# A decoder block on one core: the output is turned back on TensorE, and the projection stage goes from three pairs of PSUM banks to two

## What is computed

```
mod = silu(c) @ w_ada + b_ada          # shift, scale and gate, twice
h   = rms_norm(x) * (1 + scale1) + shift1
out_a = sparse attention(h)            # (512, 512)
out_b = gated linear recurrence(h)     # (512, 512)
merged = sigmoid(gate_a) * (out_a @ w_proj_a) + sigmoid(gate_b) * (out_b @ w_proj_b)
x   = x + gate1 * (merged @ w_out)
h2  = rms_norm(x) * (1 + scale2) + shift2
y   = square(relu(h2 @ w_mlp1 + b_mlp1)) @ w_mlp2 + b_mlp2
return x + gate2 * y                   # (1, 512 tokens, 1024 channels)
```

## Time and profile before

| | us |
|---|---|
| median of 3 runs | 870.14 |
| lowest and highest | 869.37, 870.98 |
| the profiled execution, its own time | 870.14 |
| its span in the profile | 868.3 |
| TensorE busy in the span | 827.7 (95%) |
| VectorE busy | 460.3 (53%) |
| ScalarE busy | 324.6 (37%) |

### The profile page before, as it was taken

The page is one execution under the profiler, slowest core; times in us unless marked ns, Lnnn a source line. Parts: engine busy times, 40 slices in busy tenths (PEclk is TensorE's granted clock), DMA queues, the critical chain, the costliest instruction groups (busy, mean ns, idle before and its releaser), DMA issues.

```text
span 868.3 us, 10841 instructions
## 1 busy us (share of the span) xinstructions
PE 827.7 (95%) x3919; PEld 666.8 (77%) x3919; DVE 460.3 (53%) x714; ACT 324.6 (37%) x495; POOL 222.1 (26%) x127
## 2 busy tenths in 40 slices
PE   2699899989999999999999989999999999999998
PEld 1567667878878887676888878888888888888886
DVE  3942478995788976667596656942111122220000
ACT  2643525244253335656433234444111144441110
POOL 4023423440000000000000205544444434445440
PEclk9789989999999999999999989999999999999999
DMA  9913312331222223245474722733333333333320
GB/s 353 293 52 92 97 49 73 88 90 40 74 51 56 65 73 98 79 134 153 123 226 145 232 73 81 234 97 97 97 97 97 97 97 97 97 97 97 97 97 25
DMA packets 141625, 95.74 MB, mean 110 GB/s; under 512 B 8214, under 2 KB 134804, under 8 KB 140564
## 3 DMA queue, kind: packets, MB, share of 16 engines
q1 hardware_dynamic: 140032, 95.05, 37.0%
q10 hardware_dynamic: 1556, 0.20, 0.2%
HBM read 93.13 MB, written 2.10 MB: 110 GB/s over the span
## 4 chain that ended last, share of the span: by engine, by line
PE 82%; DVE 12%; ACT 3%; issue 1%; DMA 1%; ACTq 1%; DVEq 0%
PE bank L1272 17%; PE bank L1273 17%; PE bank L1274 17%; PE bank L1422 3%; PE bank L1424 3%; PE bank L1423 3%; DVE score L980 3%; DVE top L978 3%; PE bank L1442 2%; PE bank L1614 2%; PE bank L1615 2%; PE bank L1616 2%; PE bank L1396 2%; PE bank L1300 2%; DVE rt_k L940 2%; PE bank L1398 1%
## 5 line engine op out<-in xcount | busy, mean ns | idle before, releaser
L439 POOL TENSOR_TENSOR w_lo<-w_raw,w_hi 128x1024 fp32r<-128x1024 f32 x82 | 203.5, 2483 | 322.3 <-ACT w_hi L510 322.3
L1272 PE MATMUL bank<-h_hi,w_hi 128*128 128x512 f32 x464 | 184.8, 398 | 5.3 <-DVE h_lo L918 4.8
L1273 PE MATMUL bank<-h_lo,w_hi 128*128 128x512 f32 x464 | 182.5, 393 | 0.0
L1274 PE MATMUL bank<-h_hi,w_lo 128*128 128x512 f32 x464 | 182.4, 393 | 0.0
L510 ACT ACTIVATE w_hi<-w_raw 128x1024 fp32r<-128x1024 f32 x126 | 132.6, 1052 | 133.0 <-PE bank L1274 121.4
L1272 PEld LDWEIGHTS bank<-h_hi,w_hi 128*128 128x128 f32 x464 | 88.2, 190 | 29.6 <-issue 7.6
L1274 PEld LDWEIGHTS bank<-h_hi,w_lo 128*128 128x128 f32 x464 | 88.2, 190 | 18.7
L1273 PEld LDWEIGHTS bank<-h_lo,w_hi 128*128 128x128 f32 x464 | 88.3, 190 | 17.9 <-issue 0.2
L1272 PE MATMUL bank<-u_hi,w_hi 128*128 128x512 f32 x256 | 99.7, 389 | 0.0
L1274 PE MATMUL bank<-u_hi,w_lo 128*128 128x512 f32 x256 | 99.6, 389 | 0.0
L1273 PE MATMUL bank<-u_lo,w_hi 128*128 128x512 f32 x256 | 99.6, 389 | 0.0
(11 more groups left out here) (231 smaller groups left out, 1207.4 us busy)
## 6 DMA issues: line engine op xcount, KB each, us to landing
w_raw<-in_w_mlp SPq DMA_DIRECT2D x128, 256.0 KB, 3.0
w_raw<-in_w_in SPq DMA_DIRECT2D x88, 256.0 KB, 3.4
ada_raw<-in_w_ada SPq DMA_DIRECT2D x8, 1024.0 KB, 9.0
ada_even<-in_w_ada SPq DMA_DIRECT2D x16, 512.0 KB, 4.6
ada_odd<-in_w_ada SPq DMA_DIRECT2D x16, 512.0 KB, 4.6
w_raw<-in_w_out SPq DMA_DIRECT2D x16, 256.0 KB, 3.2
x_nat<-in_x SPq DMA_DIRECT2D x4, 512.0 KB, 6.2
w_raw<-in_w_proj_a SPq DMA_DIRECT2D x8, 256.0 KB, 3.9
```

Source lines behind the costliest of these rows:

```text
L439: nc.gpsimd.tensor_tensor(w_lo[:, s], w_raw[:, s], w_hi[:, s].bitcast(F32), ALU.subtract).then_inc(lo_ready, 1)
L1272: mm(bank[b][:], w_hi[:, slot, j], rhs_hi(i), start=f, stop=False)
L1273: mm(bank[b][:], w_hi[:, slot, j], rhs_lo(i), start=False, stop=False)
L1274: end = mm(bank[b][:], w_lo[:, slot, j], rhs_hi(i), start=False, stop=l)
```

## The change

Two things are changed.

1. **The output.** The result tensor is now (1, 512 tokens, 1024 channels). Each of the 8 blocks of `xT` is turned by four 128x128 transposes on TensorE into bank 2 or 3 (`turn_back`), ACT copies the bank into a new buffer `o_stage` of two places (L841 of the changed kernel), and SP writes it: 128 partitions x 4 token blocks x 128 channels, so 512 pieces of 512 bytes where there were 128 rows of 2 KB. The last block is added on DVE in one piece, and ACT issues no DMA any more. `o_stage` lies in memory that nothing uses by then. The transposes of blocks 0 and 1 come after unit `j = 0` of `down(3)`, those of 2 and 3 after `j = 1`, of 4 and 5 after `j = 2`, of 6 and 7 after `j = 3`.
2. **The projection.** Banks 2 and 3 drop out of the rotation; blocks alternate between the pair 4, 5 and the pair 6, 7. `proj_taken` is gone. TensorE now asks, before block `m` from `m = 2` on, that `merged_ready` has come to `m - 1`, that is, that DVE has finished all of block `m - 2`, its `h_lo` included.

```diff
-    out_v = out.rearrange("(m p) t -> m p t", p=P)
+    out_v = out[0].rearrange("(b p) (m n) -> m p b n", p=P, n=P)
...
+        o_stage = place("o_stage", RL + 8 * KB, [P, 2, TB, P])
...
-        PROJ_BANK = [4, 6, 2]
...
-            for m in range(KC - 1):
-                sp.wait_ge(lin_evac, E_2[1] + m + 1)
-                sp.dma_start(out_v[m], xT[:, m]).then_inc(out_written, 16)
-            sp.wait_ge(lin_evac, E_2[1] + KC)
-            sp.dma_start(out_v[KC - 1][:, 0:T // 2], xT[:, KC - 1, 0:T // 2]).then_inc(out_written, 16)
-            sp.wait_ge(out_written, 16 * KC)
+            for m in range(KC):
+                sp.wait_ge(out_staged, m + 1)
+                sp.dma_start(out_v[m], o_stage[:, m % 2]).then_inc(out_written[m % 2], 16)
+            for b in range(2):
+                sp.wait_ge(out_written[b], 16 * KC // 2)
...
-            act.wait_ge(lin_evac, E_2[1] + KC + 1)
-            act.dma_start(out_v[KC - 1][:, T // 2:T], xT[:, KC - 1, T // 2:T]).then_inc(tail_written, 16)
-            act.wait_ge(tail_written, 16)
+            for m in range(KC):
+                act.wait_ge(y_turned, m + 1)
+                if m >= 2:
+                    act.wait_ge(out_written[m % 2], 16 * (m // 2))
+                nc.scalar.activation(o_stage[:, m % 2], bank[2 + m % 2][:].rearrange("p (b n) -> p b n", b=TB),
+                                     ACT.Copy).then_inc(out_staged, 1)
...
             for m in range(KC):
                 dve.wait_ge(group_done, G[U_P + m + 1])
-                b = PROJ_BANK[m % 3]
+                b = 4 + 2 * (m % 2)
                 sa, sb, mh, ml = sig_a[:, m], sig_b[:, m], h_hi[:, m], h_lo[:, m]
                 v.tensor_tensor(sa, bank[b][:], sa, ALU.mult)
                 dve.wait_ge(sigb_ready, m + 1)
-                v.tensor_tensor(sb, bank[b + 1][:], sb, ALU.mult).then_inc(proj_taken, 1)
-                dve.wait_ge(proj_taken, m + 1)
+                step(v.tensor_tensor(sb, bank[b + 1][:], sb, ALU.mult))
...
-                        for t in ((slice(0, T // 2), slice(T // 2, T)) if m == KC - 1 else (slice(0, T),)):
-                            v.scalar_tensor_tensor(out=xT[:, m, t], in0=bank[m % 2][:, t], scalar=GATE2[:, m:m + 1],
-                                                   in1=xT[:, m, t], op0=ALU.mult, op1=ALU.add
-                                                   ).then_inc(lin_evac, 1)
+                        v.scalar_tensor_tensor(out=xT[:, m], in0=bank[m % 2][:], scalar=GATE2[:, m:m + 1],
+                                               in1=xT[:, m], op0=ALU.mult, op1=ALU.add).then_inc(lin_evac, 1)
...
             for m in range(2, KC):
-                if m >= 3:
-                    pe.wait_ge(proj_taken, m - 2)
+                pe.wait_ge(merged_ready, m - 1)
                 pe.wait_ge(lo_ready, U_P + m + 1)
...
-            down(3)
+            def turn_back(m):
+                pe.wait_ge(lin_evac, E_2[1] + m + 1)
+                if m >= 2:
+                    pe.wait_ge(out_staged, m - 1)
+                for b in range(TB):
+                    end = nc.tensor.transpose(bank[2 + m % 2][:, b * P:(b + 1) * P],
+                                              xT[:, m, b * P:(b + 1) * P], ident[:])
+                end.then_inc(y_turned, 1)
+
+
+            for j in range(4):
+                down(3, (j,))
+                for m in (2 * j, 2 * j + 1):
+                    if m < KC - 2 or j == 3 and m < KC - 1:
+                        turn_back(m)
+            turn_back(KC - 1)
```

More of the change, by code:

```diff
@@ L235, in hybrid_block @@
             sem("sqo_ready"), sem("sqo_added"), sem("orow_summed"), sem("orow_ready"), sem("orow_spread"))
-        proj_taken = sem("proj_taken")
         sigb_ready = sem("sigb_ready")
@@ L239, in hybrid_block @@
         u_hi_ready = sem("u_hi_ready")
-        out_written, tail_written = sem("out_written"), sem("tail_written")
+        y_turned, out_staged = sem("y_turned"), sem("out_staged")
+        out_written = [sem("out_written0"), sem("out_written1")]
         assert G[U_1[0]] % 2 == 0 and G[U_1[1]] % 2 == 0
@@ L1609, in proj_blocks @@
                 n = U_P + m
-                b = PROJ_BANK[m % 3] + j0 // AC
+                b = 4 + 2 * (m % 2) + j0 // AC
                 rhs_hi, rhs_lo = (oa_hi, oa_lo) if j0 < AC else (ob_hi, ob_lo)
@@ L1779 @@
                                    kind="ExternalInput").ap())
-    _, T, D = inputs["x"].shape
-    out = nc.dram_tensor("out", (D, T), F32, kind="ExternalOutput").ap()
+    out = nc.dram_tensor("out", inputs["x"].shape, F32, kind="ExternalOutput").ap()
     hybrid_block(nc, *args, out)
-    res = run_bass_kernel_spmd(nc, [arrays], core_ids=[0]).results[0]["out"]
-    return np.ascontiguousarray(np.asarray(res).T)[None]
+    return run_bass_kernel_spmd(nc, [arrays], core_ids=[0]).results[0]["out"]
```

## The result

| | before | changed |
|---|---|---|
| median of 4 runs, us | 869.75 | 880.32 |
| lowest and highest, us | 868.19, 870.98 | 876.76, 881.94 |
| profiled execution: own time, span | 870.14, 868.3 | 883.44, 881.7 |
| span behind TensorE's last 512-column matmul | 3.08 | 4.93 |

The changed kernel takes 1.0117 times as long, 95% interval 1.008 to 1.0155. The forecast was 880.2. The profiled execution of the changed kernel, 883.44, lies above its four timed ones, 13.3 us over that of before where the medians are 10.6 apart. Where these 13.3 us lie is read stage by stage, against the earlier trace rows.

The account below looks back on a forecast made before the run. TensorE, busy 827.7 of 868.3 us, was taken to bound the kernel. Stall 3.7, clock 1.6, transposes 2.8 and tail 2.0 sum to 10.1 us; 870.14 + 10.1 = 880.2 us, 8-in-10 range 877.4 to 882.9.

Parts of the forecast that it names:

- rival D: Behind the projection: some later wait of TensorE absorbs the stall, giving 874.9 us; chance 0.04.
- The stall: Projection, block 2: TensorE waits for `merged_ready` and starts at 429.6 instead of 426.02, costing 3.7 us with the restart.
- 1.0 for the banks: Projection, block 2: a wait only until block 0's banks are read would hold it for 1.0 us.
- The forecast margin: Projection, from block 4 on: VectorE finishes 0.3 to 0.5 us ahead each time, so TensorE waits no further.
- The clock: After the projection's pause: the granted clock falls to 0.50 for 3.4 us, costing 1.6 us, bounds 0 and 3.2.
- Rival A: Projection: the clock holds after the pause, as after 2.1 us at L1300, giving 878.6 us; chance 0.16.
- Rival B: Projection: clock down for 6.8 us, or further waits for blocks 4 to 7, giving 881.8 us; chance 0.17.
- Rival E: Behind the projection: moved code avoids half-clock stretches, gaining more than the change costs, 871.9 us or less; chance 0.03.
- The transposes: Last stage: transposes between TensorE's matmuls are hidden by nothing and cost 2.8 us, bounds 2.5 and 3.2.
- rival C: Last stage: transposes count as idleness and the clock falls, giving 881.8 to 885.0 us; chance 0.04.
- The tail: From the last matmul to the end: 5.1 us instead of 3.08, costing 2.0 us, bounds 1.5 and 2.7.
- the forecast's own range: Whole kernel: 879.3 to 881.3 us, from the bounds of the transposes and the tail; chance 0.56.

Follow-up runs that it names:

- with the clock held up: Projection edit alone plus 14 unused matmuls ahead of the wait at block 2, against the kernel before: 875.52 us, ratio 1.0068.
- the filled pair: Changed kernel with unused matmuls in TensorE's pauses and the projection's stall, 877.95 us, against the kernel before with its pauses filled, 868.74 us.
- the filled runs: Two pairs of banks, waiting only for the banks, pauses filled with unused matmuls, 870.21 us, against the kernel before with pauses filled, 868.74 us.
- the run with half the filling: Kernel before with about half as many unused matmuls in its pauses as the filled one, against the kernel before: 863.42 us, ratio 0.9904.
- the two filled pairs: Output edit alone against the kernel before, both with pauses filled (873.85 against 868.74 us), and both with half that filling (868.79 against 863.42).

## Why the prediction was right

**What bounds it.** TensorE's queue carried both losses one for one; nothing downstream gave any of it back (rival D): the stretch from block 7 to the row sums is 47.01 us long in both kernels (505.87 - 458.86, 513.14 - 466.13).

**The stall.** 3.7 us forecast, 3.79 measured with the clock held up (3.86 in the filled pair), released by the row that was named and by no other. The wait for the banks alone cost 1.19 by the stage and 1.5 by the filled runs, where the prediction had 1.0 for the banks. So what costs is that TensorE asks for `merged_ready`, which comes 2.5 us later than `proj_taken`, and not that there are two pairs. The forecast margin of 0.3 to 0.5 us for blocks 4 to 7 held at its lower end. In the changed kernel VectorE finishes block 2 at 443.19 + 0.68 = 443.87, 0.30 us before TensorE begins block 4 at 444.17:

```profile
443.19 0.68 DVE L1196 TENSOR_TENSOR h_lo<-sig_a,h_hi 128x512 fp32r<-128x512 f32 x1
...
444.17 0.39 PE L1613 MATMUL bank<-ob_hi,w_hi 128*128 128x512 f32 x1
```

It is 0.29 to 0.30 for blocks 5 to 7 too, so another 0.3 us of VectorE's work per block would use it up.

**The clock.** 1.6 forecast, 1.39 measured. It fell in both profiles with the unfilled stall and didn't in both with the filled one. Rival A did not come, as far as two profiles say. The row that spoke for it was itself a matter of the execution: behind the same pause of 2.15 us the clock held in the profile of before and fell in that of the changed kernel (window 98:104 above), in code that is the same. Rival B came in a form that I had not described. Before has 6.8 us at half at the second norm, which the prediction left out; both profiles with the unfilled stall have 10.2 there, worth 1.5 us (360.91 - 359.35). The norm is unfilled in four more profiles, which have no such stall, and all four have 6.8. Whether the stall causes that is open, since similar differences come and go in unchanged code. Rival E did not come either: the changed kernel's profile has more half-clock stretches than before, not fewer. That avoiding them can be worth as much as 8 us was shown only by the run with half the filling.

**The transposes.** 2.8 forecast, 2.84 measured (2.72 and 2.74 in the two filled pairs), and rival C did not come. The Trainium skill's rule that a transpose does not keep the clock up as a matmul does (TensorE: Matmul & The Clock Gate, Part 4) was not borne out here: the clock was at 1.00 around each batch of eight. Sixteen in a row had not lowered it either; no run here has more of them.

**The tail.** 2.0 forecast, 1.85 measured. The landing of 512-byte pieces was 2.3 us for the last pair and not 2.5. That is nearer the stores of 2 KB rows (2.0) than the loads in 512-byte pieces (3.0); those loads came in pairs, so no run separates the direction of a transfer from its company. The Trainium skill (DMA: Bandwidth & Descriptors, Specifications) has 512 bytes as enough for the line rate; the trace agrees to within 0.3 us, 2.3 against 2.0 for 256 KB. TensorE took up the block 0.06 us after the addition (877.62 against 877.56) where 0.15 to 0.2 had been taken.

**The sum.** 3.79 + 1.39 + 2.84 + 1.85 = 9.9 us against 10.1 forecast and 10.6 by the medians (7.0 to 13.5 by the interval). The lower end of the forecast's own range is 879.4 by the bounds given (880.2 less 0.3 and 0.5), not 879.3. That the median met the forecast within 0.2 us is partly luck: the two medians carry a scatter of several us each, which the prediction spoke of only as a matter of the new pause. That scatter, and not the sum of terms, set how wide an honest range had to be; mine, 5.5 us wide, held the median but not all of the runs (876.76 to 881.94, the profiled one 883.44).

## What to carry to other kernels

When a buffer is dropped from a rotation, look at which event the wait is moved to: a wait for the end of all work on a block instead of for the reading of its banks cost 3.8 us instead of 1.2, and TensorE's clock fell behind the longer pause, another 1.4. Where the scatter of a kernel is as large as an edit, compare stages of the traces, and read the granted clock of the unchanged code first. Pauses of TensorE on the critical path (here of 0.7 to 2.8 us) may be worth filling with matmuls that nothing uses, if these together are shorter than the pause: in double number they gave nearly all of it back.

## What the runs showed of the hardware that I had not expected

- One and the same code ran with and without some stretches at half clock, of 3.4 us each. One starts at about 342 us, behind 4 us of matmuls of 64 rows (L1575) in which TensorE pauses for less than 0.2 us in all. It is in 4 of the 6 profiles without filled pauses and in 3 of the 6 with them, so a pause is not what it takes. What decides was not settled.
- These stretches make up much of the scatter: 28 runs of before span 6.1 us, 12 runs with the pauses filled 1.7, and the kernel with half the filling is 8.6 us faster, more than the 6 to 7 expected.
- A float32 matmul of 512 columns (`ones` by `xT`) takes 0.87 to 0.9 us at full clock in two records; the split ones take 0.227.
